# The TensorE program of the two MLP stages: four unrolled passes become a hardware loop of four turns

## The chip, the cores and the metric

The kernel runs on one core of one Trainium2 chip. The metric is the device time of one execution in microseconds (us), the median of several runs.

## What is computed

A trunk of two layers is run over 288 tokens: 256 of a prompt and 8 sequences of 4 sample tokens. Each layer has a token mixer (HGRN2 in layer 0, gated linear attention, GLA, in layer 1) and a squared-ReLU MLP, each followed by a layer norm. The change concerns the MLP:

```python
h = x * (1.0 + sc2) + sh2
y = jnp.square(jax.nn.relu(h @ w_up[l])) @ w_down[l]      # (2048 -> 8192 -> 2048)
x = layer_norm(ALPHA * x + (1.0 + g2) * y, ln_w[l, 1], ln_b[l, 1])
```

shift, scale and gate come from a projection of the conditioning vectors by w_ada (called "ada" below).

## The kernel before

The five engines run programs of their own, written by hand and synchronised by semaphores. Weights are streamed from HBM in tiles of 512 rows by 256 columns (512 KB). A tile goes through four hands: SyncE (SP) issues its load into one of 8 slots of `raw`; ScalarE (ACT) rounds it into `w_hi` (L933); VectorE (DVE) writes the rest into `w_lo` (L1330) and counts up `lo_ready`; TensorE (PE) multiplies. Both `w_hi` and `w_lo` have four slots. A tile costs TensorE 24 matmuls of 128 x 128 weights by 288 tokens: 4 row blocks, 2 column blocks, and 3 products each (high by high at L462, high by low at L463, low by high at L464). Each matmul has a weight load of its own, so a tile is 48 instructions of TensorE.

The stages follow one another: ADA0 (first part of the ada projection), HG (8 turns of 16 tiles), HGO (output projection, 32 tiles), layer norm, MLP0, layer norm, LOW (4 tiles), GLA (4 turns of 24 tiles), GLO (output projection, 32 tiles, with the rest of the last GLA turn between its first tiles), layer norm, MLP1, layer norm, output. An MLP stage is 4 passes of 64 tiles; a pass computes 2048 of the 8192 hidden features in 32 tiles and multiplies them by `w_down` in 32 more. Four tiles make a panel, the panels alternate between two pairs of PSUM banks. MLP0 also multiplies 48 ada tiles in each pass (L472) and turns their sums (L480).

On SP, ACT and DVE the four passes of an MLP stage are a hardware loop already (on the latter two, MLP1 is a loop of three and a last pass written out). On TensorE, HG is a loop (L725, turns 1 to 7) and GLA is a loop (L901, turns 1 to 3), but each MLP stage is written out four times, so that its instructions lie in a row in memory and all values that it waits for are constants.
`gemm` waits at the first tile of a panel for the panel's banks to be free (`panel_read`), then for `lo_ready`. In the first pass the first four tiles also wait for their part of the input (`a_ready`, written by the layer norm's engines). Tiles 32 to 35 wait for the hidden features (`act_ready`).

The trace names TensorE's sequencer instructions (register operations, separate semaphore waits, branches) PEldq, matmuls PE and weight loads PEld.

Of the kernel before, what the change touches and what calls it, by code (L numbers as in the profile page):

```python
# [176 lines left out]
def build_program(nc, A):  # L177
# [264 lines left out]
    def _(pe):  # L442
        mm, turn = nc.tensor.matmul, nc.tensor.transpose

        def gemm(st, n, g, p, t, x_hi, x_lo, blocks=(0, 1), between=None):

            if t == 0:
                free = st.bank_free(n, p)  # L450
                if free:
                    pe.wait_ge(panel_read[free[0]], free[1])
            pe.wait_ge(lo_ready, st.tile(n, g) + 1)
            slot = st.split_slot(g)
            for k in range(4):
                kb = 4 * t + k
                if k == 2 and between:
                    between()
                for j in blocks:
                    out = main[:, st.bank(p) + j, 0:T]  # L460
                    hi, lo = (w[:, slot, k, j * P:(j + 1) * P] for w in (w_hi, w_lo))
                    mm(out, hi, x_hi[:, kb, :], start=kb == 0, stop=False)  # L462
                    mm(out, hi, x_lo[:, kb, :], start=False, stop=False)  # L463
                    last = mm(out, lo, x_hi[:, kb, :], start=False, stop=kb == KB - 1)  # L464
            last.then_inc(tile_done, 1)

        def ada(st, n, i, kb, bank, col, first):

            slot, count = st.ring(n, "a", i)
            pe.wait_ge(raw_loaded[slot], 16 * count)  # L470
            for j in range(4):
                last = mm(bank[32 * j:32 * j + 32, col:col + 256], c_t[:, kb, :], raw[:, slot, j * 256:(j + 1) * 256],  # L472
                          start=first, stop=kb == KB - 1, skip_group_check=True, tile_position=(0, 32 * j))
            last.then_inc(ada_used, 1)

        def ada_turn(count, places, src):

            pe.wait_ge(ada_copied, count)
            for i, place in enumerate(places):
                last = turn(place, src[:, i * P:(i + 1) * P], ident[:, :])  # L480
            last.then_inc(ada_turned, 1)
# [220 lines left out]
            mm(b4[:, 0:T], ones[:, :], rstd[:, :], start=True, stop=True).then_inc(ln_var, 1)  # L702

        def mlp(st, event, with_ada):
            for n in range(st.iters):
                for s in range(64):
                    if n == 0 and s < 4:
                        pe.wait_ge(a_ready, 4 * event + s + 1)
                    if 32 <= s < 36:
                        for kp in (1, 2):  # L710
                            pe.wait_ge(act_ready, act_base[event] + 8 * n + 2 * (s - 32) + kp)
                    up = s < 32
                    gemm(st, n, s, s // 4, s % 4, *((a_hi, a_lo) if up else (act_hi, act_lo)))
                    if with_ada and s in st.ada:
                        kb, c = divmod(s, 3)
                        if s == 0:
                            pe.wait_ge(mod_ready, 12 + n)

                        ada(st, n, s, kb, (b4, b4, b5)[c], (0, 256, 0)[c], kb == 0 and c != 1)
                    if with_ada and s == 52:  # L720
                        ada_turn(13 + n, [b6[:, i * P:(i + 1) * P] for i in range(4)] +
                                 [b7[:, i * P:(i + 1) * P] for i in range(2)], mlp_b["ada"])
# [4 lines left out]
        out_projection(HGO, lambda s: hg_step(HG_PAIRS, s, False, True), 1)  # L727
        layer_norm(0, 2)
        mlp(MLP0, 2, True)
        layer_norm(1, 3)  # L730

# [171 lines left out]
        out_projection(GLO, lambda s: gl_step(GLA_HEADS, s, False, True), 4)  # L903
        layer_norm(2, 5)
        mlp(MLP1, 5, False)
        layer_norm(3, None)

# [1007 lines left out]
```

## Time and profile before

| | us |
|---|---|
| median of 3 runs | 3407.23 (3405.97 to 3408.41) |
| the profiled execution | 3408.41 |
| its span, first to last instruction | 3406.5 |
| TensorE busy in the span | 3254.7 |
| one MLP0 pass on TensorE | 241.72 |
| one MLP1 pass on TensorE | 204.36 |

The profiled execution is 1.18 us above the median, and 1.91 us of it lie outside the span. Of the profile, the page gives busy time by engine and the clock in tenths of full speed; a row of a windows view gives the stretch, its length, then busy us and instruction count of PE, PEld, DVE, ACT and POOL, then the granted clock, the share of the 16 DMA engines and GB/s; a timeline row gives start, length, engine, line, operation, tiles, count, and in brackets the idle time before it with what ended it. A row of the source view gives count, then minimum/median/maximum duration in ns, and first and last start in us.

### The profile page before, as it was taken

To read this page: it belongs to the slowest core of one execution; us is meant where nothing else is said; L and a number is where in the kernel's file an instruction comes from. 1 tells how busy PE (TensorE), PEld (TensorE's weight loads), DVE (VectorE), ACT (ScalarE), POOL (GpSimd) and SP (SyncE) were. 2 spreads that over 40 slices of the span, in tenths; PEclk is the share of its full clock that TensorE was granted. 3 is DMA by queue.
4 is the path that set the end of the run, shared out by engine and by line. 5 is a ranking of instruction groups with operands and counts; after the bars stand their busy time and mean duration, and the time that the engine had idled before them with its cause. 6 is when DMAs were issued, how large, how long until landed. Compare 5 with 4: busy or idle time off the path is not lost.

```text
span 3406.5 us, 64554 instructions
## 1 busy us (share of the span) xinstructions
PE 3254.7 (96%) x25412; PEld 2997.9 (88%) x25412; DVE 1738.0 (51%) x2375; ACT 1299.6 (38%) x1678; POOL 298.4 (9%) x306
## 2 busy tenths in 40 slices
PE   6899999998899999999999799999889999999998
PEld 2599998988788988988989699999889999999997
DVE  1466666665543434444434556556455445454444
ACT  0444444443433332332332444344235334343333
POOL 0011111110300000000001211011012000000001
PEclk7899999998899999999999899999799999999999
DMA  8967777773388688688787455654444555555552
GB/s 336 338 213 234 230 224 230 239 230 108 118 274 268 201 267 268 203 264 252 218 267 234 138 154 178 205 182 149 138 138 149 167 163 165 167 165 163 167 164 75
DMA packets 536799, 685.27 MB, mean 201 GB/s; under 512 B 21409, under 2 KB 468441, under 8 KB 536281
## 3 DMA queue, kind: packets, MB, share of 16 engines
q1 hardware_dynamic: 481090, 626.15, 58.3%
q10 hardware_dynamic: 55488, 55.91, 5.2%
q8 instruction: 171, 2.80, 0.3%
q14 instruction: 50, 0.41, 0.0%
HBM read 651.30 MB, written 30.67 MB: 200 GB/s over the span
## 4 chain that ended last, share of the span: by engine, by line
PE 88%; DVE 3%; DMA 3%; ACT 3%; issue 2%; SPq 0%; POOL 0%; ACTq 0%; DVEq 0%; POOLq 0%
PE main L462 26%; PE main L463 24%; PE main L464 24%; PE bank L472 5%; DMA raw<-in_w_ada 2%; PE bank L830 2%; PE bank L559 2%; PE bank L754 1%; PE bank L599 1%; ACT w_hi L933 1%; PE bank L836 1%; DVE z L1614 1%; DMA raw<-in_hg_w_in 1%; DVE a_lo L1335 1%; ACT ln_h L947 0%
## 5 line engine op out<-in xcount | busy, mean ns | idle before, releaser
L1330 DVE TENSOR_TENSOR w_lo<-raw,w_hi 128x1024 fp32r<-128x1024 f32 x804 | 987.5, 1229 | 1370.0 <-ACT w_hi L933 1366.1
L933 ACT ACTIVATE w_hi<-raw 128x1024 fp32r<-128x1024 f32 x804 | 850.9, 1060 | 1733.2 <-PE main L464 1667.0
L462 PE MATMUL main<-a_hi,w_hi 128*128 128x288 f32 x4368 | 1339.2, 307 | 51.9 <-DVE a_lo L1335 43.1
L463 PE MATMUL main<-a_lo,w_hi 128*128 128x288 f32 x4368 | 1303.2, 298 | 0.0
L464 PE MATMUL main<-a_hi,w_lo 128*128 128x288 f32 x4368 | 1302.2, 298 | 0.0
L462 PEld LDWEIGHTS main<-a_hi,w_hi 128*128 128x128 f32 x4368 | 835.4, 191 | 132.5 <-issue 82.1
L463 PEld LDWEIGHTS main<-a_lo,w_hi 128*128 128x128 f32 x4368 | 835.2, 191 | 4.3 <-issue 1.7
L464 PEld LDWEIGHTS main<-a_hi,w_lo 128*128 128x128 f32 x4368 | 834.5, 191 | 0.0
L462 PE MATMUL main<-act_hi,w_hi 128*128 128x288 f32 x2048 | 614.4, 300 | 0.0
L463 PE MATMUL main<-act_lo,w_hi 128*128 128x288 f32 x2048 | 604.2, 295 | 0.0
L464 PE MATMUL main<-act_hi,w_lo 128*128 128x288 f32 x2048 | 603.5, 295 | 0.0
L462 PEld LDWEIGHTS main<-act_hi,w_hi 128*128 128x128 f32 x2048 | 384.3, 188 | 28.0 <-issue 28.0
L463 PEld LDWEIGHTS main<-act_lo,w_hi 128*128 128x128 f32 x2048 | 384.5, 188 | 0.0
L464 PEld LDWEIGHTS main<-act_hi,w_lo 128*128 128x128 f32 x2048 | 384.4, 188 | 0.0
L472 PE MATMUL bank<-raw,c_t 128*32 128x256 f32 x3072 | 249.9, 422 | 18.9 <-DMA raw<-in_w_ada 18.5
L472 PEld LDWEIGHTS bank<-raw,c_t 128*32 128x32 f32 x3072 | 75.2, 113 | 112.1 <-DMA raw<-in_w_ada 59.6
L1817 POOL TENSOR_TENSOR mu<-z 128x288 f32<-128x288 f32 x4 | 3.2, 811 | 1719.2 <-DVE z L1572 1719.2
L1797 POOL TENSOR_TENSOR hg_suf<-hg_suf,hg_pre 128x256 f32<-128x256 f32 (+1 forms) x64 | 64.1, 1002 | 655.9 <-ACT hg_x L1000 655.9
L1817 POOL TENSOR_TENSOR mu<-mu,z 128x288 f32<-128x288 f32 x56 | 61.5, 1098 | 283.3 <-DVE z L1572 281.1
L1565 DVE SCALAR_TENSOR_TENSOR z<-main,mod,z 128x256 f32<-128x256 f32 x160 | 69.7, 477 | 17.1 <-PE main L464 17.1
L1698 DVE SCALAR_TENSOR_TENSOR gl_s<-gl_s,gl_dec,bank 128x512 f32<-128x512 f32 x64 | 45.0, 745 | 61.2 <-PE bank L836 60.8
L830 PEld LDWEIGHTS bank<-gl_qd,gl_s 128*128 128x128 f32 x512 | 69.1, 215 | 4.6 <-issue 4.4
(251 smaller groups left out, 2065.5 us busy)
## 6 DMA issues: line engine op xcount, KB each, us to landing
raw<-in_w_ada SPq DMA_DIRECT2D x384, 512.0 KB, 4.2
raw<-in_w_up SPq DMA_DIRECT2D x256, 512.0 KB, 3.9
raw<-in_w_down SPq DMA_DIRECT2D x256, 512.0 KB, 3.5
raw<-in_hg_w_in SPq DMA_DIRECT2D x128, 512.0 KB, 6.3
raw<-in_gla_w_in SPq DMA_DIRECT2D x100, 512.0 KB, 3.8
raw<-in_hg_w_out SPq DMA_DIRECT2D x32, 512.0 KB, 3.5
gl_s<-in_state_gla ACTq DMA_DIRECT2D x32, 512.0 KB, 4.9
out_new_gla_sample<-gl_s ACTq DMA_DIRECT2D x32, 512.0 KB, 3.2
```

Of the source, the lines that this page charges most:

```text
L462: mm(out, hi, x_hi[:, kb, :], start=kb == 0, stop=False)
L463: mm(out, hi, x_lo[:, kb, :], start=False, stop=False)
L464: last = mm(out, lo, x_hi[:, kb, :], start=False, stop=kb == KB - 1)
L472: last = mm(bank[32 * j:32 * j + 32, col:col + 256], c_t[:, kb, :], raw[:, slot, j * 256:(j + 1) * 256], start=first, stop=kb == KB - 1, s ...
L559: last = mm(bank[:, (2 * h + t) * P:(2 * h + t + 1) * P], lhs[:, h, c], rhs[:, h, c], start=True, stop=True)
L830: last = mm(b7[:, 32 * v + TB * b:32 * v + TB * (b + 1)], gl["s0"][:, slot, j, v * P:(v + 1) * P], gl["qd"][:, j, TB * b:TB * (b + 1)], st ...
L933: F(w_hi[:, st.split_slot(g)].rearrange("p k n -> p (k n)"), raw[:, slot, :], ACT.Copy).then_inc(hi_ready, 1)
L1330: V.tensor_tensor(w_lo[:, s].rearrange("p k n -> p (k n)"), raw[:, slot, :], w_hi[:, s].rearrange("p k n -> p (k n)").bitcast(F32), ALU.su ...
L1565: V.scalar_tensor_tensor(out=z[:, kb, 0:TP], in0=src[:, i, 0:TP], scalar=mod[:, layer, gate * KB + kb, 0:1], in1=z[:, kb, 0:TP], op0=ALU.m ...
L1698: last = V.scalar_tensor_tensor(out=gl["s1"][:, b % 2, j, :], in0=gl["s0"][:, b % 4, j, :], scalar=gl["dec"][:, j, b:b + 1], in1=bank[:, : ...
L1797: nc.gpsimd.tensor_tensor(suf1, suf1, last_of(pre2), ALU.add).then_inc(pool_step, 1)
L1817: add = nc.gpsimd.tensor_tensor(mu[:, :], first, z[:, kb, :], ALU.add)
```

## The change

In the TensorE program alone, the MLP's outer loop over passes becomes a hardware loop. The four waits for `a_ready` at the head of a pass are now in the loop's body, so every turn executes them, with the same constants. Everything else in the body is the same text; what depends on `n` becomes a register's value.

```diff
         def mlp(st, event, with_ada):
-            for n in range(st.iters):
+            with pe.Fori(0, st.iters) as n:
                 for s in range(64):
-                    if n == 0 and s < 4:
+                    if s < 4:
                         pe.wait_ge(a_ready, 4 * event + s + 1)
                     if 32 <= s < 36:
                         for kp in (1, 2):
```

`mlp` is called for MLP0 and for MLP1, both with `iters` of 4: two loops, each with three jumps back and one fall through.

## Rows read from the trace of the kernel before

**Rows 1.** The page: busy time, TensorE's clock in 40 slices, first lines of the chain

```profile
PE 3254.7 (96%) x25412; PEld 2997.9 (88%) x25412; DVE 1738.0 (51%) x2375; ACT 1299.6 (38%) x1678; POOL 298.4 (9%) x306
...
PEclk7899999998899999999999899999799999999999
...
PE main L462 26%; PE main L463 24%; PE main L464 24%; PE bank L472 5%; DMA raw<-in_w_ada 2%; PE bank L830 2%; PE bank L559 2%; PE bank L754 1%; PE bank L599 1%; ACT w_hi L933 1%; PE bank L836 1%; DVE z L1614 1%; DMA raw<-in_hg_w_in 1%; DVE a_lo L1335 1%; ACT ln_h L947 0%
```

**Rows 2.** Waits of TensorE over the span: total us, times, longest us

```profile
PE main L462 <- DVE a_lo L1335: 43.1, 10, 7.8
...
PE main L462 <- issue: 0.8, 2, 0.5
```

**Rows 3.** Windows: one turn each of HG, GLA, MLP0 and MLP1

```profile
352.69:434.93 82.24, 80.82 (x701) 74.12 (x700) 55.08 (x98) 39.24 (x65) 14.26 (x16) 0.98 0.73 230
2141.55:2261.19 119.64, 118.53 (x906) 113.11 (x906) 69.30 (x95) 48.81 (x75) 14.69 (x16) 0.99 0.59 181
1167.83:1409.55 241.72, 241.72 (x1928) 214.02 (x1927) 100.42 (x118) 78.41 (x82) 0.00 (x0) 1.00 0.80 244
2765.75:2970.12 204.37, 204.37 (x1538) 204.37 (x1537) 99.81 (x112) 77.72 (x80) 0.00 (x0) 1.00 0.53 165
```

**Rows 4.** Source view of the HG loop's branch, then each of the GLA loop's three

```profile
L725 PEldq COMPARE_BRANCH  x7: 76/208/256, 270.5 to 762.4; - x7
...
L901 PEldq COMPARE_BRANCH  x1: 4353/4353/4353, 2141.5 to 2141.5; - x1
...
L901 PEldq COMPARE_BRANCH  x1: 4191/4191/4191, 2261.2 to 2261.2; - x1
...
L901 PEldq COMPARE_BRANCH  x1: 83/83/83, 2380.7 to 2380.7; - x1
```

**Rows 5.** Timeline of PE: last matmul before, first after GLA's two jumps

```profile
2145.19 0.45 PE L464 MATMUL main<-a_hi,w_lo 128*128 128x288 f32 x1
2146.18 0.40 PE L462 MATMUL main<-a_hi,w_hi 128*128 128x288 f32 x1 [0.54 <-issue]
...
2265.02 0.34 PE L464 MATMUL main<-a_hi,w_lo 128*128 128x288 f32 x1
2265.64 0.40 PE L462 MATMUL main<-a_hi,w_hi 128*128 128x288 f32 x1 [0.29 <-issue]
```

**Rows 6.** MLP1, pass 0: a wait before tile 33, first matmuls of tiles 32 and 33

```profile
L453 PEldq EVENT_SEMAPHORE  x1: 51/51/51, 2662.6 to 2662.6; - x1
...
2661.77 0.29 PE L462 MATMUL main<-act_hi,w_hi 128*128 128x288 f32 x1
...
2664.97 0.30 PE L462 MATMUL main<-act_hi,w_hi 128*128 128x288 f32 x1
```

**Rows 7.** Instruction DMA (packets, MB, share) in 270:786, 2141.55:2381 and 926:1893

```profile
q8 instruction: 1, 0.02, 0.0%
...
q8 instruction: 18, 0.29, 0.5%
...
q8 instruction: 61, 1.00, 0.4%
```

**Rows 8.** Windows: two idle stretches of TensorE and what follows each

```profile
129.10:131.10 2.00, 0.34 (x3) 0.10 (x1) 1.30 (x2) 2.00 (x3) 0.00 (x0) 1.00 1.04 305
131.10:141.10 10.00, 9.93 (x98) 8.12 (x99) 4.56 (x4) 2.57 (x3) 0.00 (x0) 1.00 1.03 329
2448.50:2452.50 4.00, 0.34 (x3) 0.10 (x1) 2.77 (x6) 2.11 (x2) 0.00 (x0) 1.00 0.01 4
2452.80:2456.20 3.40, 3.40 (x16) 3.40 (x16) 0.83 (x1) 0.00 (x0) 0.00 (x0) 0.50 0.42 140
```

**Rows 9.** Windows: the first tiles of GLO and the tiles that follow

```profile
2394.80:2432.30 37.50, 36.65 (x155) 35.72 (x155) 11.52 (x19) 2.60 (x3) 0.00 (x0) 0.50 0.45 150
2432.30:2448.50 16.20, 16.05 (x110) 15.09 (x110) 6.84 (x7) 6.51 (x11) 0.00 (x0) 1.00 0.46 162
```

**Rows 10.** Timeline of PE: the first matmul of MLP1

```profile
2557.80 0.61 PE L462 MATMUL main<-a_hi,w_hi 128*128 128x288 f32 x1 [7.18 <-DVE a_lo L1335]
```

## The prediction

> **What bounds the kernel now.** I read the page first. TensorE is busy 96% of the span and its three matmul lines make up three quarters of the chain that ended last; no other engine is above 51% [rows 1]. Its waits come next: they are few, the largest is for the layer norms' output, and none falls into an MLP pass after its first tile. The windows of one turn of each stage show that directly: in both MLP stages TensorE is busy for the whole turn, 241.72 of 241.72 us and 204.37 of 204.37, at clock 1.00 [rows 3]. One MLP1 pass is 64 x 24 = 1536 matmuls, so a matmul goes every 204.36 / 1536 = 0.133 us. Whatever delays TensorE's stream there is paid in full, and nothing in the stage can be sped up by register values in place of constants. So two questions are left: what does a jump back cost, and how much of it do the instructions cover that TensorE already holds?
>
> **The jump.** The trace has two loops on TensorE to read it from. The HG loop's branch took 208 ns (76 to 256), the GLA loop's taken branches 4353 and 4191 ns, its last, not taken, 83 ns [rows 4]. What tells them apart is the body's length. An HG turn is 701 + 700 = 1401 matmuls and weight loads, a GLA turn 906 + 906 = 1812, an MLP0 turn 3855 and an MLP1 turn 3075 [rows 3]. And in the HG loop's 516 us one instruction packet was fetched, in two GLA turns 18, in unrolled MLP0 61 of 16 KB each [rows 7]: HG's body stays in TensorE's instruction memory, GLA's does not, and a jump to its head has to wait for a fetch. Both MLP bodies are longer than GLA's, so I take the GLA price for them. The Trainium skill says the same from the other side (Runtime: NRT & Kernel Launch, Instruction fetch mechanics): a taken branch whose target is not held forces a DMA fetch before execution goes on. The same skill's Advanced Engine Details and Errata (Control Flow Timing) puts a compare-and-branch at about 108 ns, and six at that price would add 0.65 us at most; the 4191 and 4353 ns rows go against using it here.
>
> From the branch to the first matmul of the next turn: 2146.18 - 2141.55 = 4.63 us and 2265.64 - 2261.19 = 4.45 us [rows 3 to 5] (the windows of rows 3 begin and end at these branches). That holds the branch and the register work behind it.
>
> **The cover.** TensorE's sequencer runs ahead of its matmuls. In MLP1 the wait in front of tile 33 was handled at 2662.60, and tile 33's first matmul started at 2664.97 [rows 6]: 2.37 us, or 17.8 matmuls of 0.133 us. The branch comes some 0.1 us after the add before it, so it finds 2.37 - 0.10 = 2.27 us of matmuls to cover it. GLA is a check. There the last queued matmul began at 2145.19, at a pitch of 0.24 us, and the first of the next turn at 2146.18, so 0.75 us were lost; at the second jump 2265.64 - 2265.02 - 0.24 = 0.38 us. TensorE was at half clock there, which made the cover longer, 4.63 - 0.75 = 3.88 and 4.45 - 0.38 = 4.07 us, about 16 to 17 matmuls of 0.24 us. In the MLP the clock is full, so the same number of matmuls covers little more than half of that.
>
> Loss per jump: 4.45 - 2.27 = 2.18 to 4.63 - 2.27 = 2.36, I take 2.27 us. Two loops of four turns make six jumps: 6 x 2.27 = 13.6 us. The two falls through (83 ns) are covered.
>
> **The other parts.**
> - Register operations in each tile: one to four per tile of 3.2 us, in the sequencer, behind the 2.27 us cover. In the whole span TensorE waited for issue twice, 0.8 us in total, which are the two GLA jumps themselves [rows 2, 5]; in the HG and GLA loops every tile has such operations and none shows as a wait. Nothing; without cover they would cost some 0.1 us a tile.
> - The `a_ready` waits in turns 1 to 3: long satisfied, nothing.
> - The `a_ready` wait in turn 0: before, tile 0's weight load itself waits, 7.18 us in MLP1 [rows 10]. With a register value to work out for `lo_ready`, the wait can move to the sequencer, and the first load follows only after it. Bounds: nothing, and 4.63 - 4.35 = 0.28 us, the register work behind a jump. I take 0.2 for each of two stages: 0.4 us.
> - Instruction traffic: the bodies are still fetched in every turn, nothing gained or lost on DMA.
> - ACT, DVE and SP are untouched. Their buffers are full during a stall, so when TensorE resumes its tiles are ready; nothing is late next but the rest of the program.
>
> Sum on the profiled execution: 3406.5 + 1.9 + 13.6 + 0.4 = 3422.4; on the median, which is 1.2 us lower, 3421.2. **I say 3421.**
>
> **The clock, both ways.** A stall is also idle time, and the granted clock may fall. After a gap of 2.0 us with three matmul ends in it the clock stayed at 1.00 (2.4 GHz); after 4.0 us it was 0.50 (1.2 GHz) for 3.4 us, with 16 matmuls in place of some 26, so 10 x 0.133 = about 1.4 us lost [rows 8]. My 2.27 us stall is nearer to the first, so I take no drop; the other end is six drops, +8 us, which gives 3429. In GLO the clock was 0.50 for 37.5 us, with 155 matmuls; the next 16.2 us at 1.00 had 110, or 0.147 us each [rows 9]. At that pace the 155 take 22.8 us, so 14.7 us hang on when the clock comes back. GLO lies after MLP0, and a delay moves its matmuls against whatever makes the chip decide.
>
> **The rivals.**
> 1. GLO's clock recovers early because MLP0 ends some 7 us later. For it: HGO, the same code in layer 0, is not at half clock for so long (the slices around its place on the page are 8 [rows 1]). Against: the idle time that starts it is untouched, and the three runs lie within 2.5 us. Price -14.7, so 3421.2 - 14.7 = 3406.5. This is the case that is not slower; it outweighs the jumps as soon as more than 14.0 us are regained.
> 2. The jump costs as in HG, 0.21 us: covered tenfold, 3407 to 3408. It needs the 3855 and 3075 instruction bodies to stay in a memory that did not hold 1812. Almost excluded for the branch itself, but something else in GLA (a slow fetch beside its state loads) could have made those two long.
> 3. The queue covers the jump. By the Trainium skill (Advanced Engine Details and Errata, Engine Queue Depths) TensorE's queue holds 64 instructions. As a mechanism of this kernel: if 32 pairs of load and matmul were held, the cover would be 32 x 0.133 = 4.26 us, a jump would lose 4.54 - 4.26 = 0.28 us, and six 1.7 us: 3409. The 17.8 matmuls of rows 6 and the 16 to 17 at the GLA jumps speak against it.
> 4. Jumps cost more: a second fetch is late too when a body's head lies close to the end of a fetched block, or MLP0's 0.80 share of busy DMA (GLA 0.59 [rows 3]) delays the fetch. Up to one more fetch of 4.2 us at three of the jumps, +12.6, or six clock drops, +8: 3429 to 3434.
>
> **Chances.** Forecast (jumps of about 2.3 us, clock terms small or cancelling, 3414 to 3431) 0.60; rival 1 in full or in large part (3400 to 3414) 0.24; rivals 2 and 3 together 0.08; rival 4 above 3431 0.08. The range 3406 to 3432 leaves out half of rival 1 and rival 4's upper part. This kernel's measurement tells a change of about 0.2%, 6.8 us. Slower by more (above 3414): 0.60 + 0.08 = 0.68. Within: 0.20 of rival 1 and the 0.08 of rivals 2 and 3 = 0.28. Faster: 0.04 from rival 1, with all of its gain and cheap jumps.
>
> **What would show it.** Right: six new COMPARE_BRANCH entries of 4 to 4.5 us at the MLP's loop line and two of 0.08; a gap of 2.2 to 2.4 us in TensorE's starts at the head of turns 1 to 3 of each MLP stage, put down to issue; MLP1's turns 206.6 us in place of 204.36, MLP0's 244.0 in place of 241.72. Wrong: branches of 0.2 us (rival 2), long branches without gaps (rival 3), a GLO that is shorter (rival 1), gaps above 3 us or a half clock behind each (rival 4).

## The result, and the profile after

The changed kernel took 3434.28 us (median of 4 runs, 3433.54 to 3440.26) against 3407.62 us: ratio 1.0082, 95% interval 1.0067 to 1.0096, or some 27 us slower. Measured again later, it took 3425.51 us (median of 6 runs, 3423.97 to 3435.09), ratio 1.0068, interval 1.0052 to 1.0083. The forecast was 3421, so the direction was right and the first median lies 2 us above the range. The profiled execution, from which the rows below are taken, has a span of 3423.6 us, 17.1 us longer than that of the kernel before. That is shorter than every timed run of the first measurement (their spans are 3429.6 to 3438.4 us) and like the quick runs of the second (3422.1 to 3423.7 us), so the rows explain a quick run and not the first median.

The source view of the loop line, `mlp`'s L705, and of single jumps in it:

```profile
L705 PEldq COMPARE_BRANCH  x8: 83/3947/4217, 1164.7 to 3390.1; - x8
...
L705 PEldq COMPARE_BRANCH  x1: 4200/4200/4200, 1164.7 to 1164.7; - x1
...
L705 PEldq COMPARE_BRANCH  x1: 3600/3600/3600, 1410.3 to 1410.3; - x1
...
L705 PEldq COMPARE_BRANCH  x1: 4114/4114/4114, 1653.8 to 1653.8; - x1
...
L705 PEldq COMPARE_BRANCH  x1: 3967/3967/3967, 2765.8 to 2765.8; - x1
...
L705 PEldq COMPARE_BRANCH  x1: 4217/4217/4217, 2973.8 to 2973.8; - x1
...
L705 PEldq COMPARE_BRANCH  x1: 3927/3927/3927, 3182.1 to 3182.1; - x1
```

Six jumps took 3.6 to 4.2 us each, as GLA's did before [rows 4]. The timeline of PE shows the gap behind the first, the second and the fourth; the other three are like them:

```profile
1166.80 0.29 PE L464 MATMUL main<-act_hi,w_lo 128*128 128x288 f32 x1
1169.22 0.39 PE L462 MATMUL main<-a_hi,w_hi 128*128 128x288 f32 x1 [2.12 <-issue]
...
1412.42 0.29 PE L464 MATMUL main<-act_hi,w_lo 128*128 128x288 f32 x1
1414.24 0.39 PE L462 MATMUL main<-a_hi,w_hi 128*128 128x288 f32 x1 [1.52 <-DVE mlp_zs L1568]
...
2767.94 0.29 PE L464 MATMUL main<-act_hi,w_lo 128*128 128x288 f32 x1
2770.11 0.39 PE L462 MATMUL main<-a_hi,w_hi 128*128 128x288 f32 x1 [1.89 <-DVE mlp_zs L1568]
```

From start to start these are 2.42, 1.82 and 2.17 us where 0.13 is the pitch. (The view names VectorE's L1568 as what ended two of them. The branch record ends 0.36 us before each of those matmuls, and the hinted loop below, with the same waits for banks, has no gap there; so it was the branch that held TensorE, and the releaser that the view names is a bystander.) The six gaps, each less one pitch, are 2.29, 1.69, 2.19, 2.04, 2.29 and 2.01: 12.5 us together.

What a turn lost is more than its gap. Windows from branch to branch, MLP0's three turns and MLP1's three, to be set beside 241.72 and 204.37 [rows 3]:

```profile
1164.70:1410.30 245.60, 243.48 (x1928) 215.55 (x1928) 100.41 (x118) 78.37 (x83) 0.00 (x0) 0.99 0.77 241
1410.30:1653.80 243.50, 241.98 (x1929) 214.06 (x1928) 100.41 (x118) 78.40 (x83) 0.00 (x0) 1.00 0.79 242
1653.80:1899.30 245.50, 243.47 (x1929) 215.55 (x1928) 100.86 (x118) 78.41 (x83) 13.09 (x13) 0.99 0.78 240
2765.80:2973.80 208.00, 206.11 (x1538) 205.89 (x1537) 99.82 (x112) 77.69 (x81) 0.00 (x0) 0.99 0.53 163
2973.80:3182.10 208.30, 206.17 (x1538) 205.94 (x1537) 99.77 (x112) 77.64 (x81) 0.00 (x0) 0.99 0.54 162
3182.10:3390.10 208.00, 206.16 (x1538) 205.93 (x1537) 97.36 (x110) 74.86 (x78) 15.13 (x13) 0.99 0.46 140
...
1170.10:1173.50 3.40, 3.40 (x17) 3.40 (x16) 0.04 (x1) 0.00 (x0) 0.00 (x0) 0.51 0.00 0
1414.80:1418.20 3.40, 3.40 (x31) 2.82 (x29) 0.95 (x1) 0.49 (x1) 0.00 (x0) 1.00 0.10 34
2770.90:2774.30 3.40, 3.40 (x17) 3.40 (x16) 0.38 (x1) 0.00 (x0) 0.00 (x0) 0.50 0.46 131
```

Five of the six turns are 3.6 to 3.9 us longer than before, one is 1.8. The last three rows say why: behind the first and the fourth jump TensorE ran at half clock (0.51, 0.50) for 3.4 us, with 17 matmuls; behind the second, after the shortest gap, the clock stayed at 1.00. So a turn loses its 2.0 to 2.3 us of idle time and about 1.5 us of half clock, or, once, 1.7 us of idle time alone. Over the six turns: 1358.9 - 3 x 241.72 - 3 x 204.36 = 20.7 us, of which 12.5 are idle time and 8.2 what came behind it.

In this profile the rest of the program then gave some of it back. GLO's first tiles, which had been at half clock for 37.5 us [rows 9]:

```profile
2409.00:2432.00 23.00, 22.54 (x139) 21.53 (x140) 10.69 (x17) 2.28 (x3) 0.00 (x0) 0.80 0.55 194
2432.00:2450.00 18.00, 17.86 (x96) 16.67 (x97) 5.08 (x5) 6.68 (x11) 0.00 (x0) 0.78 0.35 118
```

Matched matmul by matmul, the two traces are 6.7 us closer after GLO's first tiles than at their start, and 1.6 us further apart after the last layer norm. 20.7 - 6.7 + 1.6 leaves 1.5 us to the 17.1 of the spans: 0.7 at the start of the program, 0.7 in the layer norm behind MLP0, 0.7 less in GLA, and the rest in small parts.

### The profile page after: what moved, and what is told of

Its sections match the earlier page's. It is cut to its first block, busy times and chain, and to the rows that moved or that the text cites. A ratio compares the mean times of both kernels' runs of the same rounds, so it can differ in the third digit from the quotient of the medians.

```text
span 3423.6 us, 65170 instructions
## 1 busy us (share of the span) xinstructions
PE 3257.8 (95%) x25412; PEld 2999.5 (88%) x25412; DVE 1738.4 (51%) x2375; ACT 1299.5 (38%) x1678; POOL 297.2 (9%) x306
## 4 chain that ended last, share of the span: by engine, by line
PE 88%; DVE 4%; ACT 3%; DMA 3%; issue 2%; SPq 0%; POOL 0%; ACTq 0%; DVEq 0%; POOLq 0%
PE main L462 25%; PE main L463 24%; PE main L464 24%; PE bank L472 5%; DMA raw<-in_w_ada 2%; PE bank L559 2%; PE bank L830 2%; PE bank L754 1%; PE bank L599 1%; ACT w_hi L933 1%; DVE z L1614 1%; DMA raw<-in_hg_w_in 1%; PE bank L836 1%; DVE a_lo L1335 1%; ACT ln_h L947 0%
## 5 line engine op out<-in xcount | busy, mean ns | idle before, releaser
L1565 DVE SCALAR_TENSOR_TENSOR z<-main,mod,z 128x256 f32<-128x256 f32 x160 | 69.6, 477 | 17.1 <-PE main L464 17.1
L559 PE MATMUL bank<-hg_x 128*128 128x128 f32 x448 | 61.6, 280 | 8.2 <-DVE hg_x L1435 8.2
```

Source lines behind the costliest of these rows:

```text
L559: last = mm(bank[:, (2 * h + t) * P:(2 * h + t + 1) * P], lhs[:, h, c], rhs[:, h, c], start=True, stop=True)
L1565: V.scalar_tensor_tensor(out=z[:, kb, 0:TP], in0=src[:, i, 0:TP], scalar=mod[:, layer, gate * KB + kb, 0:1], in1=z[:, kb, 0:TP], op0=ALU.m ...
```

## The experiments

The theory after the result: a jump costs because its target has to be fetched; TensorE idles for what the queued matmuls don't cover; the idle time draws half clock behind it; nothing else in the loop costs. The rivals: the register values of the loop cost time in every tile; or the jump costs as a jump.

**Fetch the loop's head ahead of the jump.** A prefetch hint for the closing branch stands at the head of each turn:

```diff
-            with pe.Fori(0, st.iters) as n:
+            with nc.Fori(0, st.iters, 1, engines=[mybir.EngineType.PE], hint_back_edge=True) as n:
```

 Rival (register values in the waits and the loop as such cost the time, spread over the tiles): 3428 us or more, with gaps of their own. Second rival (the jumps cost their time whatever is prefetched, since the sequencer drains): branches stay near 4 us, 3425 to 3440.

Measured: 3406.86 us, ratio 0.9995 (0.9985 to 1.0004). Source view of L705, and windows inside MLP0's first two full turns:

```profile
L705 PEldq BRANCH_PREFETCH_HINT  x8: 36/38/50, 915.5 to 3171.9; - x8
...
L705 PEldq COMPARE_BRANCH  x8: 87/361/387, 1165.2 to 3375.8; - x8
...
1165.00:1407.00 242.00, 242.00 (x1931) 214.32 (x1930) 100.41 (x118) 78.68 (x83) 0.00 (x0) 1.00 0.78 244
1407.00:1649.00 242.00, 242.00 (x1931) 214.30 (x1930) 100.47 (x119) 78.59 (x83) 0.00 (x0) 1.00 0.79 244
```

The same loop, the same register values, and a body longer by one instruction; the branches take 0.36 us, TensorE is busy throughout at clock 1.00, and the loss is gone. That leaves nothing for register work, for the repeated `a_ready` waits, or for the loop as such, but for 0.2 us before each stage's first matmul (7.36 us of idle time in place of 7.18), which the changed kernel has too.

**Many short loops.** MLP1's passes are written out, but three quarters of their tiles lie in loops whose body is 8 tiles:

```python
            # cut: tiles() writes out 8 tiles; MLP0 calls it for all 64 of a pass
            for n in range(st.iters):
                for start in (0, 32):
                    tiles(n, start)
                    with pe.Fori(0, 3) as q:
                        tiles(n, start + 8, ahead=8 * q, panels=2 * q)
```

> MLP0 written out as before; each pass of MLP1 is written as tiles 0 to 7, a loop of three turns over tiles 8 to 31 (8 tiles, some 390 instructions a turn), tiles 32 to 39, and a loop of three turns over tiles 40 to 63. That is 8 loops with 16 jumps back and register values in three quarters of the tiles. Theory (only a jump to instructions that are no longer held costs): branches of 0.1 to 0.3 us, all covered, 3406 to 3410 us. Rival (any jump or register value costs): 16 jumps at 2.1 us or more, 3440 us; a spread register cost would give 3417 to 3421.

Measured: 3400.55 us, ratio 0.9985 (0.9976 to 0.9995).

```profile
L731 PEldq COMPARE_BRANCH  x24: 76/207/234, 2606.7 to 3373.1; - x24
```

Sixteen jumps at some 0.21 us, no gap, and MLP1 as long as before to 0.1 us in the trace. The jump as such is free when its target is still held. The median is 6.9 us below that of the kernel before beside it and below the bracket, and the trace has no place for such a gain: stage for stage it differs by 0.4 us at most, but for the program's first 270 us. But that trace is of a run of 3406.75 us, and eight of the twelve runs took 3399.6 to 3401.4. The kernel before has such runs too: of its 68 timed beside these experiments 15 took 3398.6 to 3401.7 us, the others 3404.2 to 3413.2. The run with the same MLP1 and one more hint, below, had the median of the kernel before, and its profile (3401.65 us) shows where a quick run gains:

```profile
2394.80:2432.30 37.50, 36.77 (x207) 35.31 (x208) 13.45 (x21) 4.60 (x7) 0.00 (x0) 0.73 0.53 187
```

This is GLO in that run, at 0.73 where [rows 9] has 0.50, with nothing ahead of it moved by more than 0.6 us; GLO is 6.7 us shorter. So GLO's clock can come back early by itself. Why it did so more often with the short loops is open.

**One stage at a time.** `mlp` uses the loop for one stage only:

```diff
+            loop = pe.Fori(0, st.iters) if st is MLP0 else None
+            for n in ([loop.__enter__()] if loop else range(st.iters)):
```

> Only MLP0 is a loop on TensorE, MLP1 is written out as before. Theory: three jumps at 2.1 us, half clock behind one to three of them at 1.5 us, so +8 to +11 us at the end of MLP0; if GLO's half clock of 37.5 us then ends early, up to 10 us of it come back, if not nothing: 3409 to 3412 or 3416 to 3420, and the trace says which. Rival (the loss is spread over the tiles by register work): +13 us, and MLP0 turns longer without a gap at their heads.

> Only MLP1 is a loop on TensorE, MLP0 is written out as before. Nothing ahead of MLP1 moves, so GLO stays as in the kernel before (half clock for 37 us). Theory: three jumps at 2.1 us and three stretches of half clock at 1.5 us, +10.8 us, and up to 2 us in the last layer norm: 3416 to 3421 us. Rival (no clock term, jumps alone): 3414 us. Rival (GLO's clock state varies by itself, without any delay ahead of it): the same gain or loss of up to 10 us shows here too.

Measured: MLP0 alone 3421.16 us, ratio 1.0033 (1.0020 to 1.0046), its runs from 3412.3 to 3427.8; MLP1 alone 3422.29 us, ratio 1.0038 (1.0026 to 1.0051). Each is near half of the whole loss and 1 us above its bracket. In the trace of MLP1 alone that stage is 11.6 us longer and the last layer norm 1.6, which stays at half clock for longer. GLO is at half clock for 30.7 us there in place of 37.5, though nothing ahead of it was changed: a small case of the second rival. In the trace of MLP0 alone (the slowest of its runs) the stage lost 11.3 us and GLO lost another 3.4: half clock for 44 us. A GLA turn has more half clock than before; the last two rows are the first matmul behind GLA's first jump and the clock soon after it.

```profile
2152.00:2280.00 128.00, 125.60 (x925) 119.00 (x925) 70.67 (x97) 48.78 (x75) 14.66 (x16) 0.95 0.57 173
2410.80:2455.00 44.20, 43.86 (x183) 42.56 (x184) 13.64 (x21) 3.83 (x5) 0.00 (x0) 0.50 0.47 159
...
2157.00 0.39 PE L462 MATMUL main<-a_hi,w_hi 128*128 128x288 f32 x1 [1.83 <-issue]
...
2158.10:2168.30 10.20, 10.20 (x35) 7.95 (x34) 3.63 (x6) 0.80 (x2) 0.00 (x0) 0.50 0.48 157
```

GLA's clock of 0.95 is to be set beside 0.99 of a turn in [rows 3]. In the kernel before, the matmuls queued ahead of this jump ran at half clock and the idle time was 0.54 us [rows 5]; here they ran at full clock, TensorE sat idle for 1.83 us, and half clock came behind it, for 10.2 us. It is the same jump, only met at another clock. I had bracketed GLO's gain but no loss in GLA; matched matmul by matmul it is 6.0 us from the start of LOW to the end of GLA's loop.

**Hold the sequencer without a fetch.** The passes are written out, and an empty loop stands at the head of passes 1 to 3. With 14, 10 and 6 turns it holds the sequencer for some 5.2, 3.7 and 2.2 us (the edit is shown for 14):

```diff
             for n in range(st.iters):
+                if n:
+                    with pe.Fori(0, 14):
+                        pass
                 for s in range(64):
```

> The kernel before, all passes written out, with an empty loop of 14 turns on TensorE's sequencer at the head of passes 1 to 3 of both MLP stages. An empty turn is an add and a short branch, an estimated 0.3 us from the HG loop's rows, so the sequencer is held for some 4.2 us, as long as by a far jump, and nothing has to be fetched. Theory (what costs is that the sequencer is held longer than the 16 to 17 queued matmuls last, and the half clock behind the idle time): gaps of 2 us at six places, half clock behind most of them, 3425 to 3436 us, as the changed kernel. Rival (the fetch itself disturbs, through DMA or a drained queue): 3407 to 3412.

> As the run with 14 empty turns, with 6: the sequencer is held for some 1.9 us at six places. Theory (2.13 us of queued matmuls cover a held sequencer): no gap, clock 1.00 throughout the MLP stages, 3404 to 3411 us. Rival (any time in which the sequencer is held costs): six times 1.9 us, 3419 us.

> The kernel before with 10 empty turns of the sequencer at the head of passes 1 to 3. The runs with 14 and 6 turns held it for some 5.2 and 2.2 us (0.37 us a turn), so 10 turns hold it for 3.7 us and TensorE idles some 1.4 us at six places. Theory (the idle time itself, and half clock only behind a stall long enough): six times 1.4 us, 8.6 us, and no half clock in the MLP stages, 3413 to 3418 us. Rival (any stall there draws half clock behind it): six times 2.9 us, 3423 to 3427.

Measured: 14 turns 3435.36 us, ratio 1.0081 (1.0064 to 1.0099); 10 turns 3423.96, 1.0051 (1.0037 to 1.0064); 6 turns 3408.45, 1.0009 (1.0000 to 1.0018). The first and the last lie in the theory's brackets. First matmul of pass 1 with 14 turns and a window behind it, then with 10 turns the same:

```profile
1168.81 0.37 PE L462 MATMUL main<-a_hi,w_hi 128*128 128x288 f32 x1 [2.73 <-issue]
...
1169.00:1173.00 4.00, 4.00 (x20) 4.00 (x20) 0.12 (x1) 0.00 (x0) 0.00 (x0) 0.57 0.00 0
```

```profile
1167.38 0.37 PE L462 MATMUL main<-a_hi,w_hi 128*128 128x288 f32 x1 [1.25 <-DVE mlp_zs L1571]
...
1167.30:1173.30 6.00, 5.92 (x47) 5.38 (x48) 2.58 (x3) 1.06 (x1) 0.00 (x0) 1.00 0.32 88
```

A held sequencer without any far jump gives the changed kernel's kind of loss: gaps, and half clock behind them. From start to start the gaps are 3.0 us with 14 turns and 1.5 with 10, so four empty turns are 1.5 us and one is 0.37; with 6 turns, 2.2 us, there is none. The cover is 14 x 0.37 - 2.9 = 2.3 us, close to the prediction's 2.27. Half clock came behind each of the six gaps of 3.0 us and behind none of the six of 1.5.

With 10 turns the median lies 6 us above my bracket, though the clock in the MLP stages is as the theory says. Its profile (3417.65 us, the quickest of its runs) shows where such time goes: MLP0 and MLP1 lost 8.9 us, LOW and GLA 5.9 (in the way that the run with MLP0 alone shows), the last layer norm 1.6, and GLO gave back 6.7. The other runs have no profile; that GLO gave nothing back in them would give about their time, but isn't shown.

**A second late block.** The loops' heads are placed late in a fetched block:

```diff
-            with pe.Fori(0, st.iters) as n:
+            with nc.Fori(0, st.iters, 1, engines=[mybir.EngineType.PE], head_slot={mybir.EngineType.PE: 230}) as n:
```

> The changed kernel with the two MLP loops' first instruction placed at slot 230 of a block of 256 fetched instructions, so that 26 instructions (13 matmuls, 1.7 us) behind the head the next block is needed too. Theory: that block is fetched only after the jump, so a second wait of 0.5 to 4 us falls into each turn's first tiles: gaps in two places, 3440 to 3465 us. Rival (the two blocks are fetched at once): no second gap, 3430 to 3440.

Measured: 3446.25 us, ratio 1.0120 (1.0102 to 1.0137). Timeline at the head of MLP1's second and third jumps:

```profile
3002.56 0.40 PE L462 MATMUL main<-a_hi,w_hi 128*128 128x288 f32 x1 [2.19 <-issue]
3005.86 0.30 PE L464 MATMUL main<-a_hi,w_lo 128*128 128x288 f32 x1 [1.58 <-issue]
...
3210.82 0.39 PE L462 MATMUL main<-a_hi,w_hi 128*128 128x288 f32 x1 [1.88 <-DVE mlp_zs L1568]
3214.37 0.30 PE L464 MATMUL main<-a_hi,w_lo 128*128 128x288 f32 x1 [1.83 <-issue]
```

A second gap follows the first, six times, of 0.5 to 2.0 us less one pitch, and the time is 21 us above that of the changed kernel measured beside it. Most of that is not in the MLP stages, though: their six turns lost 27.1 us in this profile, where the changed kernel's lost 20.7 and 23.6. GLA's two turns lost 14.4 us. GLA's jumps have a second gap here as well, with half clock behind it:

```profile
2161.00 0.40 PE L464 MATMUL main<-a_hi,w_lo 128*128 128x288 f32 x1 [2.23 <-issue]
...
2161.40:2171.60 10.20, 10.20 (x35) 7.94 (x34) 3.26 (x5) 0.25 (x1) 0.00 (x0) 0.50 0.51 157
```

Moving the MLP loops' heads also moves all code behind them; that GLA's loop came to lie badly by it would explain this, but no run here shows it. So a second late block as in rival 4 of the prediction occurs, but not in the changed kernel, where each jump has one gap.

**The changed kernel again.**

> The changed kernel again, for more times and one more profile. Six jumps at 2.1 us of gap, 12.6, half clock of 3.4 us behind most of them, 1.5 us each, up to 9, and about 2 us in the last layer norm: 3426 to 3436 us. If GLO is at half clock for some 20 us or less in the profile its time is below 3428; if for 30 us or more, above 3430.

Measured: 3425.51 us, 0.5 below the bracket. In its profile the branches took 4.0 to 4.7 us, the gaps less one pitch are 2.1 to 2.8 us and 13.8 together, and the six turns lost 23.6 us, so that 9.8 came behind the gaps. Half clock stands behind all six jumps, and a window of GLO is at 0.77:

```profile
2404.60:2450.00 45.40, 44.04 (x252) 41.88 (x253) 16.72 (x25) 9.11 (x13) 0.00 (x0) 0.77 0.51 172
```

Six runs fall into two groups, 3423.97 to 3425.55 (four) and 3433.22 to 3435.09 (two), some 9 us apart. Both profiles of the changed kernel are of such quick runs and have GLO's clock back early. That the upper group, and with it the first measurement's 3434, is the one with GLO at half clock for long fits 6.7 us of the 9 and was not seen in a profile of this kernel. The profile with 14 empty turns (3438.12 us) is the nearest: six gaps, half clock behind each, and GLO at 0.50 for 37.5 us.

**Hints on GLA too.** The hint on the GLA loop, with hinted MLP loops, with written-out MLP passes, and with the short loops:

```diff
-        with pe.Fori(1, GLA_HEADS) as n:
+        with nc.Fori(1, GLA_HEADS, 1, engines=[mybir.EngineType.PE], hint_back_edge=True) as n:
```

> The prefetch hint on the MLP loops and on the GLA loop too, whose two far jumps cost 1.1 us of gap together in the kernel before. Theory: GLA's branches 0.4 us, no gap there, 1.1 us less than the hinted MLP loops, 3403 to 3409 us. Rival (a moved phase of GLO's half clock outweighs it): 3398 to 3402 or 3408 to 3414.

> The kernel before, MLP passes written out, with the hint on the GLA loop alone. Theory: 1.1 us less than the kernel before between 2141 and 2270 us, 3403 to 3409 us, hardly to be told from it. Rival (as above): 3398 to 3402 or 3408 to 3414.

> MLP1 in short loops as before in this study, and the hint on the GLA loop. The short loops' trace showed MLP1 as long as in the kernel before to 0.1 us; its lower median came with a start that was 1 to 2 us shorter. Theory: that was chance of the start, so this is the kernel before less 1.1 us, 3403 to 3409. Rival (short loops really gain, by less instruction fetching): 3398 to 3401.

Measured: 3400.28 us, ratio 0.9983 (0.9974 to 0.9992), with the hinted MLP loops; 3407.41, 0.9997 (0.9988 to 1.0006), with written-out passes; 3407.22, 0.9997 (0.9988 to 1.0006), with short loops. The last two are as the theory said; the first is 3 us below it, in the first rival's range. Source views of GLA's branch in the first two:

```profile
L901 PEldq COMPARE_BRANCH  x3: 80/216/233, 2140.8 to 2378.7; - x3
```

```profile
L901 PEldq COMPARE_BRANCH  x3: 87/4072/4306, 2142.8 to 2382.0; - x3
```

The hint worked on GLA only together with hinted MLP loops. There the whole turn stayed held: 6 instruction packets from 2022 to 2379 us against 25 in the kernel before. Why it didn't work without them, where the branches still took 4 us (with the short loops too, 3892 and 4106 ns), is open; the GLA loop also lies at another place in memory in that kernel, and the experiments don't separate the two. The kernel with all hints is 7 us faster than the one before. In its profile the two GLA turns are 1.3 us shorter, and GLO's first tiles 8.2. Between the two TensorE now waits where it had not waited, in the last GLA turn, and no longer waits for VectorE's `gl_ksm` (4.2 us before, 0.4 now), behind which GLO's long half clock had begun:

```profile
PE bank L830 <- issue: 1.9, 1, 1.9
...
PE bank L830 <- DVE gl_ksm L1690: 0.4, 2, 0.2
```

All eleven runs of this kernel took 3397.5 to 3402.0 us, so here the early clock came every time. That it came from this moved wait is likely and not shown.

## Why the prediction was right and wrong

- **What bounds the kernel**: right. TensorE was busy for whole MLP turns and every delay there was paid.
- **The jump**: right. 3.6 to 4.2 us in the first profile and 4.0 to 4.7 in the second, where GLA had 4.2 and 4.35. The hint and the short loops show that the fetch is the cause, not the branch. Rival 2 is out. That a body of 1812 can't be held is too strong: with all hints GLA's was.
- **The cover**: right. 17 matmuls still began after each branch had started, 2.3 us of them; the empty loops give 2.3 us too. Rival 3, with twice the queue, is out: its jumps would have lost 0.3 us.
- **The loss per jump**: 2.27 us forecast, 1.7 to 2.3 measured in one profile and 2.1 to 2.8 in the other, 12.5 and 13.8 us for six where I had 13.6.
- **Registers, waits, traffic at nothing**: right, by the hinted loop's time and its 242.00 of 242.00 us; the first load's 0.2 us for each stage is there too. One reading was not: the wait view of the kernel before has a third wait for issue, 1.4 us at L593 at 790.3 us, behind the HG loop's end. It changes no term.
- **The clock**: this is the term that failed. "My 2.27 us stall is nearer to the first, so I take no drop". Of six stalls five drew half clock in one profile and six in the other, at about 1.6 us each, 8.2 and 9.8 us where I put 0. The two rows that I chose between [rows 8] are a single case each, and taking the nearer one for a stall between them gave 0 where the bound of six drops, +8 us, was the truth. I also compared unlike measures: from start to start the two gaps are 2.03 and 4.00 us, and my stall is 2.40, with its pitch. The runs since have many cases: no half clock behind six gaps of 1.5 us and one of 1.8, but behind all of the eleven gaps of 2.1 us and more in the changed kernel's two profiles. With the head at slot 230 two gaps of 2.2 and 2.5 us drew none, so the length of the gap does not settle it alone.
- **GLO, rival 1**: GLO's clock came back early in both profiles of the changed kernel and gave 6.7 us, less than the 14.7 of its full price. But rival 1's reason, the later end of MLP0, isn't shown: the short loops with the hint have the same 6.7 us without a delay, and the kernel before has quick runs of its own. I had left out that a shift can also cost: up to 6 us in GLA, 3.4 us in GLO and 1.6 us in the last layer norm.
- **The sum**: 12.5 of idle time, 8.2 of clock and 1.6 of layer norm are 22.3 us, or 3430. With the second profile's terms, 13.8 and 9.8, and 1.3 and 1.6 for the layer norms behind MLP0 and MLP1, it is 26.5 us, or 3434, the first median, if GLO gives nothing back. That is an estimate; there is no profile of a run at 3434. The second median, 3425.5, lies in the range that I gave, but by luck: the clock term that I left out and GLO's gain, which my sum had at nothing too, nearly cancel there.

## What to carry to other kernels

A hardware loop on TensorE is free as long as its body stays in the engine's instruction memory: here 1401 matmuls and weight loads did, and 1812 did not but in the kernel with all hints. Beyond that each turn pays 4.0 to 5.1 us from the branch to the next matmul, less what is queued (2.3 us of full-pitch matmuls), unless a prefetch hint for the closing branch stands at the loop's head and works; and on an engine that bounds the kernel, price the half clock behind the stall as well as the stall. Look in the trace for the branch's own record; the wait views can name bystanders. And when a median moves by 7 us, look first whether the runs fall into two groups.

## What the runs showed that I had not expected

- Gaps of 2.1 to 3.0 us in dense matmuls drew half clock behind them for 3.4 us, in one case 6.8, though not always: the two gaps of 2.49 and 2.18 us at MLP1's last jumps in the run with the head at slot 230 had a second gap close behind and no half clock. What came behind TensorE's idle time added two thirds to it.
- Stages whose code nobody touched changed by more than a jump costs, through the granted clock: GLA by up to +6.0 us behind a delayed MLP0, GLO's first tiles by -6.7 us (its 0.50 [rows 9] became 0.80 and 0.78) and by +3.4. GLO's clock also came back early without a delay, which is likely what parts the runs of one kernel into two groups.
- The prefetch hint made a 4 us jump 0.36 us in the MLP loops, had no effect on GLA's by itself (4072 and 4306 ns), and kept GLA's whole body held when the MLP loops had it too (216 and 233 ns).
